# Memory gemms inside the sparse attention: whole panels in every second step in place of half panels in each

## What is computed

```python
x = x + 0.5 * swiglu(rms_norm_2(x, ...), ...)
q, k, v, q_idx, k_idx, w_idx, ... = split(h @ w_in[l])
y_a = conformer_conv(...)            # 31 taps, layer norm, swish
y_b = short_gated_conv(...)          # 3 taps
y_c = dsa_attention(q, k, v, ...)    # 8 heads, 4 blocks of 128 queries, top 128 keys of the causal ones
x = x + concatenate([y_a, y_b, y_c]) @ w_out[l]
k, v = split(mem_n @ wkv)            # keys and values of the memory: 256 rows, 16 panels of 128 columns
x = x + memory_cross_attention(...)
x = x + 0.5 * swiglu(...)
```

## Time and profile before

| what | value |
|---|---|
| median of three executions | 3587.68 us (3587.47 to 3589.31) |
| the profiled execution, its own time | 3595.74 us |
| its span, first to last instruction | 3593.9 us |
| granted TensorE clock, mean | 0.982 of full |
| TensorE busy | 3448.0 us, 96% |
| VectorE busy | 1964.1 us, 55% |
| ScalarE busy | 1361.3 us, 38% |

### The profile page before, as it was taken

One profiled execution on the slowest core, in us unless ns is written; L12 is line 12 of the kernel. 1 busy time (PEld: TensorE's weight loads), 2 busy tenths in 40 slices (PEclk: granted clock), 3 DMA queues, 4 the chain that ended last, 5 costly groups with the idle time before them and its releaser, 6 DMA issues.

```text
span 3593.9 us, 41967 instructions
## 1 busy us (share of the span) xinstructions
PE 3448.0 (96%) x15492; PEld 2781.0 (77%) x15492; DVE 1964.1 (55%) x2679; ACT 1361.3 (38%) x1916; POOL 213.3 (6%) x158
## 2 busy tenths in 40 slices
PE   7999999999999999998998999999999989999999
PEld 5778777778888888876776888888887777768887
DVE  4667754455446545578653544464446974444444
ACT  3454433432224332345543322242223564343223
POOL 1000000000000000026200000000000640000000
PEclk9999999999999999999999999999999999999999
DMA  3333312223233333332221333333333221213332
GB/s 124 89 87 84 93 48 59 72 92 109 95 104 94 94 94 94 89 93 71 71 78 40 94 97 102 88 100 94 105 88 94 76 78 59 82 48 102 97 94 82
DMA packets 425594, 310.27 MB, mean 86 GB/s; under 512 B 17256, under 2 KB 423200, under 8 KB 425440
## 3 DMA queue, kind: packets, MB, share of 16 engines
q1 hardware_dynamic: 422880, 302.13, 28.2%
q0 software_dynamic: 1664, 4.52, 0.4%
q10 hardware_dynamic: 896, 1.54, 0.1%
HBM read 306.06 MB, written 2.10 MB: 86 GB/s over the span
## 4 chain that ended last, share of the span: by engine, by line
PE 87%; DVE 8%; ACT 3%; issue 2%; DMA 0%; ACTq 0%; DVEq 0%; POOL 0%
PE G L664 77%; PE G L805 2%; DVE w_lo L1809 1%; DVE arena L1662 1%; PE B L653 1%; ACT w_hi L1113 1%; DVE small L1661 1%; PE G L653 1%; PE B L530 1%; PE B L571 1%; PE B L609 1%; PE G L512 1%; PE B L878 0%; DVE y_lo L1824 0%; PE B L777 0%
## 5 line engine op out<-in xcount | busy, mean ns | idle before, releaser
L1113 ACT ACTIVATE w_hi<-raw 128x1024 fp32r<-128x1024 f32 x579 | 613.7, 1060 | 1596.3 <-PE G L664 1563.2
L664 PE MATMUL G<-xn_hi,w_hi 128*128 128x512 f32 x2848 | 1133.9, 398 | 17.5 <-DVE w_lo L1809 16.5
L1809 DVE TENSOR_TENSOR w_lo<-raw,w_hi 128x1024 fp32r<-128x1024 f32 x580 | 722.3, 1246 | 766.8 <-ACT w_hi L1113 764.4
L664 PE MATMUL G<-xn_lo,w_hi 128*128 128x512 f32 x2848 | 1112.4, 391 | 0.0
L664 PE MATMUL G<-xn_hi,w_lo 128*128 128x512 f32 x2848 | 1112.0, 390 | 0.0
L664 PEld LDWEIGHTS G<-xn_hi,w_hi 128*128 128x128 f32 x2848 | 537.1, 189 | 149.1 <-issue 32.3
L664 PEld LDWEIGHTS G<-xn_lo,w_hi 128*128 128x128 f32 x2848 | 537.1, 189 | 119.8 <-issue 10.2
L664 PEld LDWEIGHTS G<-xn_hi,w_lo 128*128 128x128 f32 x2848 | 536.7, 188 | 113.2
L664 PE MATMUL G<-y_hi,w_hi 128*128 128x512 f32 x1472 | 578.8, 393 | 5.2 <-DVE y_lo L1824 5.2
L664 PE MATMUL G<-y_hi,w_lo 128*128 128x512 f32 x1472 | 575.3, 391 | 0.0
L664 PE MATMUL G<-y_lo,w_hi 128*128 128x512 f32 x1472 | 575.1, 391 | 0.0
(11 more groups left out here) (362 smaller groups left out, 2826.6 us busy)
## 6 DMA issues: line engine op xcount, KB each, us to landing
raw<-in_w_in SPq DMA_DIRECT2D x128, 512.0 KB, 4.5
raw<-in_ffn_w_gate SPq DMA_DIRECT2D x88, 512.0 KB, 4.0
raw<-in_ffn_w_up SPq DMA_DIRECT2D x88, 512.0 KB, 5.2
raw<-in_ffn_w_down SPq DMA_DIRECT2D x64, 512.0 KB, 4.1
raw<-in_w_mlp_up SPq DMA_DIRECT2D x32, 512.0 KB, 4.6
raw<-in_w_mlp_down SPq DMA_DIRECT2D x32, 512.0 KB, 4.0
raw<-in_xa_wkv SPq DMA_DIRECT2D x32, 512.0 KB, 4.1
raw<-in_w_out SPq DMA_DIRECT2D x24, 512.0 KB, 4.3
```

What stands on the lines that cost most here:

```text
L664: m = pe.matmul(bank[:, 0:n], a[:, k, kt, :], b[:, kt * S:kt * S + n], start=(kt == 0 and t == 0), stop=(kt == nk - 1 and t == 2))
L1113: act.activation(w_hi[:, k], raw[:, 1 - q, :, k * P:(k + 1) * P], ACT.Copy).then_inc(s_whi, 1)
L1809: dve.tensor_tensor(w_lo[:, k], raw[:, 1 - q, :, k * P:(k + 1) * P], w_hi[:, k].bitcast(F32), ALU.subtract)\
```

## The change

In odd steps -1, 1, ..., 29 TensorE now issues both halves of one panel, i+1 and i+2, one behind the other; in even steps it issues none. Nothing else is changed: the queues of ScalarE, VectorE, GpSimd and SyncE are the same instruction for instruction, and TensorE has the same instructions in another order.

```diff
@@ -560,8 +560,9 @@
                     sums(0)
                 if i == square_step:
                     sums(1)
-                if -1 <= i <= 30:
+                if -1 <= i <= 30 and i % 2:
                     half_kv(l, i + 1)
+                    half_kv(l, i + 2)
                 if i >= 0:
                     b, hh = steps[i]
                     if hh == 0:
```

## The result

The changed kernel takes **3601.93 us** in the median, the kernel before 3588.35 (3587.47 to 3589.31), six executions each. The ratio is 1.0036, with a 95% interval of 1.0025 to 1.0048: slower by 13.0 us. The forecast was 3582.5 with a range up to 3589.0, so the sign is wrong and the time lies outside of the range.

The account below looks back on a forecast made before the run. TensorE, busy 96% of the span, was taken as the bound, so only its idle or slow time counted. Terms gave -4.7 us per layer at full clock, -2.6 with falls, -5.2 for both: 3587.68 to 3582.5, range 3577 to 3589.

Parts of the forecast that it names:

- A: Even steps: PV keeps only S as cover for its copy; cost 0, upper bound some 0.45 us per step.
- Rival 3: Slower: PV of even steps waits for its copy, up to 0.45 us each; +8.3, 3596.0; chance 0.10.
- B: Weight switches on TensorE: one S-to-half switch per pair goes, one S-to-PV comes; -0.3 us, bounds 0 and -1.5.
- C: Steps -1 to 11: `turn_out` of step 9 0.9 us late, half 11 already done (-1.54); net -0.6.
- D: Step 12 to the root: T(24) and the root's chain, so PV(27), +0.5 us; waits 1.6 before S(30), 0.9 before PV(27).
- E: PV(27) to the last `turn_out`: 13.2 us instead of 18.37, that is -5.2, about 4.5 of it the clock.
- The clock: Falls per layer: one behind the S(30) wait, 1.5 us, +0.6 after slack; about one more, +1.5; leaving -2.6.
- Rival 2: Clock falls as before or more often, since pauses only move; together -1.1 us, 3586.6; chance 0.20.

Follow-up runs that it names:

- second trace of before: The kernel before, unchanged, run again for another trace: 3588.02 us, ratio 1.0, profiled execution 3588.13.
- changed and filled: The changed kernel with extra throwaway matmuls ahead of eight waiting instructions in each attention: 3581.47 us, 0.9979.
- filled kernel before: The kernel before with 9, 16, 10, 20, 5 and 9 throwaway matmuls in its waits, none before PV(27): 3587.53 us, 0.9996.
- the 35: The changed kernel with 35 extra matmuls in one piece ahead of the first panel of each attention: 3608.0 us, 1.0054.
- the four starts: Both kernels with 0, 7, 14 or 21 extra matmuls ahead of each attention's first panel: means 3600.51 us before, 3600.31 changed.

## Why the prediction was wrong

**The waits and most of the full-clock sums held.** The table takes the time from the first matmul of the first panel to each mark and then from mark to mark, from the starts shown (first matmul at 1699.81 in the second trace of before, 1698.92 changed, 1700.24 changed and filled):

| stretch | before, 2nd trace | changed | changed, filled | the fall's cost (changed less filled) |
|---|---|---|---|---|
| to `turn_out` of step 9 | 31.09 | 33.34 | 31.85 | 1.49 |
| to `sums(0)` | 31.61 | 30.15 | 30.16 | -0.01 |
| to `sums(1)` | 11.42 | 12.98 | 11.33 | 1.65 |
| to `turn_out` of step 25 | 21.26 | 23.01 | 21.45 | 1.56 |
| to PV(27) | 10.19 | 12.07 | 10.18 | 1.89 |
| to the last `turn_out` | 13.84 | 13.38 | 13.37 | 0.01 |
| sum | 119.41 | 124.93 | 118.34 | 6.59 |

- *A, even steps lose their cover: right.* There is no idle time before PV in an even step before step 30. Rival 3, the slower one that put its loss there, is refuted, although the sign came out as it said.
- *B, switches: 0, not -0.3.* In the rows below, from the timeline of TensorE of the changed kernel, PV behind S lasts 0.95 us (1791.48 to 1792.43) where it took 0.83 behind a half: the 0.1 that the half paid is now paid by PV. It counts 0.3 us.

```profile
1790.43 1.12 PE L530 MATMUL B<-arena 64*128 64x512 f32 x2
1791.48 1.10 PE L572 MATMUL B<-arena 128*128 128x64 f32 x8
1792.43 0.61 PE L654 MATMUL G<-consts,arena 128*128 128x128 f32 x4
```

- *C, steps -1 to 11: right.* `turn_out` of step 9 stands 0.76 later at full clock (31.85 to 31.09; predicted 0.9), half 11 is gone from the next stretch (31.61 to 30.16, -1.45; -1.54). The wait of 0.71 instead of 1.1 follows. What C left out is S(10), whose wait grew from 1.18 to 1.68.
- *D, the root's chain: right.* The wait before S(30) is 1.51 (1.6), the one before PV(27) 0.89 in the filled kernel (0.9). Against the kernel before with its sums at full clock (PV(27) at 1804.25 - 1699.92 = 104.33 from the first matmul) the filled one stands at 104.97, +0.64, where +0.5 was predicted.
- *E, PV(27) to the last `turn_out`: its length right, its reference wrong.* 13.38 measured, 13.2 predicted, both new waits 0.69. But in the trace near its median the kernel before takes 13.84 and not 18.37, so E is worth -0.5 and not -5.2; the difference is the 4.5 "of the clock".

At full clock throughout, the kernel before would take 104.33 + 13.84 = 118.17 (put together from two traces) and the changed one takes 118.34. So the terms A to E, without the clock, sum to +0.2 per layer. The prediction had -4.7 + 4.5 = -0.2.

**The step that failed is "The clock".** It expected in each layer one fall behind S(30), mostly taken up by the slack before PV(27), +0.6, and one more, +1.5: 2.1. Measured are four falls of 1.49, 1.65, 1.56 and 1.89, together 6.6. The one at `sums(1)` is in the kernel before too and costs it 1.3 (from there to `turn_out` of step 25 21.26, and 19.98 in the filled kernel before), so the change adds 5.3 where 2.1 was expected. With the +0.2 of A to E that is the 5.5 by which the sums of the table differ. The four come behind the wait of 1.68 before S(10), with the granted clock at 0.65 in the 3.2 us from 1721.0 on, in `sums(0)` (3.32 us instead of 1.98), in and behind `sums(1)` (3.31 instead of 2.36), and behind the wait of 1.51 before S(30), with 0.53 for 7 us. The last was the one foreseen, and mis-sized: S(30) and the panel take 6.96 us up to PV(27) (1803.51 to 1810.47), where the filled kernel comes there 1.89 sooner with 0.89 of idle time among it. The fall takes 2.8 and not 1.5, and less the slack it is 1.9 and not 0.6.

**The second fault is the baseline.** I laid the difference of two stretches of one execution on the median, though that execution stood 8 us above it and its excess was in those very stretches. 124.1 - 2.6 = 121.5 was the forecast for an attention; it takes 125.0, 3.5 more. It was subtracted from 124.1 where 119.4 was typical, 4.7 less. Together 8.2 per layer: +5.6 measured, -2.6 predicted; the baseline is over half of it. Of the 12.6 us between the span of the changed kernel (3598.9) and that of the second trace of before (3586.3), the attentions hold 5.6 + 5.5 (windows above); the stretch between the attentions is 1.2 longer (1086.7 to 1085.5), that behind the second 1.2, and the start is 0.9 earlier.

**Is the change slower by itself?** Shown is that inside the attentions, with 11.1 of the 12.6 us, the loss is the clock: the two kernels differ there by 0.2 per layer at full clock, and with matmuls in the waits of the changed one its loss was gone and 7 us more. Shown too is that extra matmuls at the start move the kernel before by 20 us, of which at most 6.7 are their own time, and the changed one by 4 (10 with the 35), with equal waits. Over the four starts the kernels average 3600.5 and 3600.3. So the halves in each step owe their 3588 to a start at which two of their three long waits bring no fall. Rival 2, "falls as before, or more often", comes nearest to what happened; it had 3586.6, since it too counted from a trace with the fall in it. The Trainium skill, "TensorE: Matmul & The Clock Gate", section "A second HAM failure mode: psum-queue depth-cycling", tells of a kernel whose short idle times between groups of matmuls make the clock go back and forth. The traces agree with it in so far as falls stand behind waits of 1.2 to 2.6 us, all of them waits for ScalarE or VectorE.

**Open** is what fixes the moment. Waits of one length bring a fall in one kernel and none in the next, while the executions of one kernel lie within 1.2 to 8.2 us of each other, most within 5 us; the seven of before at 3596 are an exception. Only four starts were tried, and their mean has no interval worth the name. The extra matmuls at the start are work as well as delay, and no kernel with a mere delay was tried, so which of the two moves the falls is not shown. Nor was the kernel before run with its wait of 2.33 filled: at full clock its attention would take 118.17 by the sum above, and the changed one 118.34, so the 7 us that the filled changed kernel is ahead say nothing for its order. Why the stretches behind the attentions differ by 1.2 us I have not separated; in the second trace of before the 10 us behind the first one ran at 0.69, and at 1.00 in the filled kernel.

## What to carry to other kernels

Before a difference of some tenths of a per cent is put down to an order of instructions, delay the stage by a microsecond or two and measure both kernels at several delays: here 14 extra matmuls moved the kernel before by 20.4 us (0.57%), of which 13.7 or more are not their own time, as much as the change did. Compare the profiled execution with the median first, and where it is off, find the stretch that holds the excess before anything is subtracted from it. Where a latency-bound stage lets TensorE wait one or two microseconds at a time, price its falls of the clock at 1.3 to 4.7 us each and put idle matmuls into the waits, if a bank is free. Fill every long wait and read the clock again: in the kernel before one was left open, the fall moved there, and nothing was gained.

## What the runs showed of the hardware that was not expected

- 14 extra matmuls at the start of each attention (3.3 us per layer) made the kernel before 20.4 us slower with its waits equal to 0.02 us; the granted clock behind the wait of 2.10 was 0.50 for 8.6 us, where the unshifted kernel had 1.00.
- Of 98 executions of the kernel before, seven took 3595.7 to 3596.8 us and the others 3586.4 to 3590.2, with nothing between.
- Two executions of the kernel before, traced, gave 124.1 and 119.4 us for the attention of layer 0, and agreed within 0.02 us from `turn_out` of step 9 to PV(27).
- 79 matmuls per layer whose results are thrown away made the changed kernel 19.9 us faster; with three of the eight places filled it was 12.9.
- One fall cost between 1.3 us (at `sums(1)`, in the kernel before) and 4.7 us (behind the wait of 2.33 before PV(27), in the kernel before shifted by 14).
